# A three-block fp32 network: spectra swapped, maxima spread and a taps' spectrum doubled by DMA instead of TensorE

## What is computed

```python
p = h @ w_in
a_val, a_gate, z_a, q, k, v, o, z_b, gates = split_cols(p, EVEN_SIZES)
u = a_val * jax.nn.sigmoid(a_gate)
u = depthwise_conv_centred(u, conv_w, conv_b)          # 31 taps per channel
u = jax.nn.silu(group_layer_norm(u, gn_g, gn_b, A_GROUPS))
y_a = u * jax.nn.silu(z_a)
h_fwd = mlstm_chunkwise(qh, kh, vh, i_f, f_f)          # 4 heads, and again backwards
h_bwd = fl(mlstm_chunkwise(fl(qh), fl(kh), fl(vh), fl(i_b), fl(f_b)))
y = jnp.concatenate([y_a, y_b], axis=-1) @ w_out
```

## Time and profile before

| | us |
|---|---|
| three runs | 868.88, 870.31, 870.93 |
| median | 870.31 |
| the profiled execution, its time | 870.27 |
| its span on the core | 868.5 |
| PE busy | 850.9 |
| DVE busy | 500.8 |
| ACT busy | 476.6 |
| POOL busy | 38.5 |

### The profile page before, as it was taken

How to read it: one execution, slowest core, us unless ns; L and a number is a source line. 1 busy time by engine, 2 the same in 40 slices (tenths; PEclk the granted TensorE clock), 3 DMA queues, 4 the chain that set the end, 5 groups by cost and what they waited for, 6 DMA issues and landing times.

```text
span 868.5 us, 10829 instructions
## 1 busy us (share of the span) xinstructions
PE 850.9 (98%) x4078; PEld 695.5 (80%) x4078; DVE 500.8 (58%) x759; ACT 476.6 (55%) x761; POOL 38.5 (4%) x67
## 2 busy tenths in 40 slices
PE   8999899999999999999999999999999999999996
PEld 6888787888888888887788766888888887788885
DVE  6657642656666666545355644856665566546463
ACT  6557645663456555433466463438764577555551
POOL 2000000000000000810000010000000100000000
PEclk9999999999999999999999999999999999999999
DMA  8763433655466565675456514535564557265021
GB/s 270 257 190 117 146 97 98 193 172 188 129 197 216 175 186 191 175 240 189 152 178 200 169 33 162 170 98 170 171 219 155 145 171 248 73 184 192 2 97 48
DMA packets 75876, 140.36 MB, mean 162 GB/s; under 512 B 6082, under 2 KB 12517, under 8 KB 75825
## 3 DMA queue, kind: packets, MB, share of 16 engines
q1 hardware_dynamic: 72432, 134.37, 49.2%
q0 software_dynamic: 3328, 5.29, 2.2%
q10 hardware_dynamic: 64, 0.02, 0.0%
HBM read 138.56 MB, written 1.06 MB: 161 GB/s over the span
## 4 chain that ended last, share of the span: by engine, by line
PE 90%; DVE 4%; ACT 3%; issue 1%; DMA 1%; SPq 0%; DVEq 0%; ACTq 0%
PE acc L1552 25%; PE acc L1554 25%; PE acc L1553 25%; PE aux L1588 2%; PE aux L1840 2%; PE aux L1905 1%; DVE wlo L388 1%; ACT whi L534 1%; PE aux L2024 1%; PE aux L1968 1%; PE aux L1829 1%; DMA raw<-in_w_in 1%; PE aux L2032 1%; PE aux L2033 1%; PE aux L1701 1%
## 5 line engine op out<-in xcount | busy, mean ns | idle before, releaser
L388 DVE TENSOR_TENSOR wlo<-raw,whi 128x1024 fp32r<-128x1024 f32 (+2 forms) x257 | 304.7, 1203 | 228.6 <-ACT whi L534 227.9
L534 ACT ACTIVATE whi<-raw 128x1024 fp32r<-128x1024 f32 (+2 forms) x257 | 264.4, 1045 | 232.6 <-PE acc L1554 208.9
L1552 PE MATMUL acc<-whi,a_hi 128*128 128x512 f32 (+4 forms) x720 | 277.5, 385 | 3.3 <-DVE wlo L388 2.5
L1554 PE MATMUL acc<-whi,a_lo 128*128 128x512 f32 (+4 forms) x720 | 272.7, 379 | 0.0
L1553 PE MATMUL acc<-wlo,a_hi 128*128 128x512 f32 (+4 forms) x720 | 272.2, 378 | 0.0
L1552 PEld LDWEIGHTS acc<-whi,a_hi 128*128 128x128 f32 x720 | 135.8, 189 | 33.0 <-issue 5.4
L1554 PEld LDWEIGHTS acc<-whi,a_lo 128*128 128x128 f32 x720 | 135.6, 188 | 24.9
L1553 PEld LDWEIGHTS acc<-wlo,a_hi 128*128 128x128 f32 x720 | 135.8, 189 | 24.2 <-issue 0.7
L1552 PE MATMUL acc<-whi,b_hi 128*128 128x512 f32 x234 | 92.3, 395 | 0.1
L1554 PE MATMUL acc<-whi,b_lo 128*128 128x512 f32 x234 | 91.2, 390 | 0.0
L1553 PE MATMUL acc<-wlo,b_hi 128*128 128x512 f32 x234 | 91.1, 389 | 0.0
(11 more groups left out here) (334 smaller groups left out, 774.6 us busy)
## 6 DMA issues: line engine op xcount, KB each, us to landing
raw<-in_even_w_in SPq DMA_DIRECT2D x54, 512.0 KB, 4.4
raw<-in_w_in SPq DMA_DIRECT2D x50, 512.0 KB, 3.8
raw<-in_w_up SPq DMA_DIRECT2D x32, 512.0 KB, 4.5
raw<-in_w_down SPq DMA_DIRECT2D x32, 512.0 KB, 3.5
raw<-in_even_w_out SPq DMA_DIRECT2D x16, 512.0 KB, 4.1
raw<-in_odd_w_in SPq DMA_DIRECT2D x16, 512.0 KB, 4.5
raw<-in_odd_w_out SPq DMA_DIRECT2D x12, 512.0 KB, 3.7
raw<-in_w_branch_gla SPq DMA_DIRECT2D x8, 512.0 KB, 3.3
```

The source lines that it names most:

```text
L388: return e.tensor_tensor(w_view(wlo[u % SPLIT], u), w_view(raw[u % RAW], u), w_view(whi[u % SPLIT], u).bitcast(F32), ALU.subtract)
L534: act.activation(w_view(whi[u % SPLIT], u), w_view(raw[u % RAW], u), ACT.Copy).then_inc(sem("hi_done"), 1)
L1552: pe.matmul(acc_of(c, t), ah[:, ts], hi[:, k], start=first, stop=False)
L1554: ins = pe.matmul(acc_of(c, t), al[:, ts], hi[:, k], start=False, stop=last)
```

## The change

- **Taps' spectrum.** FW keeps one matrix of 128 columns (cosines, then sines). PE makes two matmuls instead of four. ACT copies rows 0 to 63 of each bank (real part) to rows 0 to 63 of WS[:, 0], rows 64 to 127 (imaginary part) to SOB and, negated, to rows 64 to 127 of WS[:, 1]. POOL issues four transfers that fill the other halves of the rows (ws_in).
- **Spectra.** ACT copies each of the three banks of a way there to `spectrum(b, 0)` (`spectra_out`). POOL issues for each block two transfers that put its halves, exchanged, into `spectrum(b, 1)` (`swap_halves`). The DVE waits for these, multiplies both by WS in SBUF and adds the second to the first (three more instructions for each n). The way back has one matrix FI and four matmuls instead of eight, and waits for `filtered`. FI's loads are halved.
- **Maxima.** POOL writes RM to the DRAM tensor `skew` and reads it back into MB on 128 partitions (1 MB; MB lies in EQT). ACT waits for it (mb_in) and reads MB instead of the banks. PE's four matmuls with 4 rows go, and "eq" is one piece.
- **Order.** The way back 1 on PE stands behind the turn of the keys; `conv_rows(1)` on the DVE behind three units of "ev1"; `filtered(1)` behind all of pump("eq"); the DVE splits one unit of "eq" ahead of `filtered(0)`; `group_rstd(1)` on ACT stands behind the copies of "ev1".

```diff
--- before.py
+++ after.py
@@ -150,10 +150,10 @@
         if STAGES >= 2:
-            AUX += [("ws", w, n) for w in range(2) for n in range(2)] + split_keys("en", 8) + [("gat", 0), ("gat", 1)]
+            AUX += [("ws", n) for n in range(2)] + split_keys("en", 8) + [("gat", 0), ("gat", 1)]
             AUX += [("fx", 0, b) for b in range(3)] + [("cvT", 0, t) for t in range(NT)] + [("mcol",)]
-            AUX += [("mb", h) for h in range(4)] + [("fx", 1, b) for b in range(3)]
-            AUX += [("eqT", 0, j) for j in range(2)] + [("cvT", 1, t) for t in range(NT)] + [("eqT", 1, j) for j in range(2)]
+            AUX += [("fx", 1, b) for b in range(3)]
+            AUX += [("eqT", w, j) for w in range(2) for j in range(2)] + [("cvT", 1, t) for t in range(NT)]
             AUX += [("kq", h) for h in range(4)]
@@ -266,18 +266,19 @@
             FT = sb("FT", [P, 4, 2 * P], c=c3)
-            FI = sb("FI", [P, 2, 4, P], c=c3)
+            FI = sb("FI", [P, 4, P], c=c3)
             cvb = sb("cvb", [P, D], c=c3)
...
             e_hi, e_lo = sb("e_hi", [P, 4, TOK], F32R, c=c3), sb("e_lo", [P, 4, TOK], F32R, c=c3)
+            MB = flat(EQT[:, :, :, :]).rearrange("p (h d t) -> p h d t", h=4, d=2)
             HM = flat(EQK[:, :, :, :]).rearrange("p (t n) -> p t n", t=NT)
...
             wcv_in = SOB[0:31, 0]
-            FW = SOB[0:31, 1, 0:512].rearrange("p (w c) -> p w c", w=2)
+            FW = SOB[0:31, 1, 0:256]
@@ -474,24 +475,42 @@
                 chain(pool.memset(FT[:, :, :], 0.0))
-                chain(pool.memset(FI[:, :, :, :], 0.0))
+                chain(pool.memset(FI[:, :, :], 0.0))
                 pool.dma_start(wcv_in, A["even_conv_w_2"][0]).then_inc(sem("wcv_in"), 16)
                 rows = A["dft_s"].rearrange("n (a c) -> n a c", a=2)
-                for a in range(2):
-                    pool.dma_start(FW[:, :, P * a:P * a + P], rows[0:31, :, 0:P]).then_inc(sem("wcv_in"), 16)
+                pool.dma_start(FW.rearrange("p (a c) -> p a c", a=2), rows[0:31, :, 0:P]).then_inc(sem("wcv_in"), 16)
                 for j, (_, p0, r0, n) in enumerate(F_ROWS):
...
                 for j, (p0, m0, n) in enumerate(I_COLS):
-                    for w in range(2):
-                        for a in range(2):
-                            pool.dma_start(FI[64 * a:64 * a + 64, w, j, p0:p0 + n], odd[0:64, 1, (a + w) % 2, m0:m0 + n]
-                                           ).then_inc(sem("fi_in"), 16)
+                    for a in range(2):
+                        pool.dma_start(FI[64 * a:64 * a + 64, j, p0:p0 + n], odd[0:64, 1, a, m0:m0 + n]
+                                       ).then_inc(sem("fi_in"), 16)
                 pool.dma_start(gbias[:, :], A["even_b_gate_2"][0].partition_broadcast(P)).then_inc(sem("gbias_in"), 16)
                 pool.dma_start(cvb[:, :], A["even_conv_b_2"][0].partition_broadcast(P)).then_inc(sem("cvb_in"), 16)
+                for n in range(2):
+                    aux_done(pool, ("ws", n))
+                    cs = slice(512 * n, 512 * n + 512)
+                    pool.dma_start(WS[64:128, 0, cs], WS[0:64, 0, cs]).then_inc(sem("ws_in"), 16)
+                    pool.dma_start(WS[0:64, 1, cs], SOB[64:128, 0, cs]).then_inc(sem("ws_in"), 16)
                 pool.wait_ge(sem("units_used"), CH[CI["dn1"]]["units"][-1] + 1)
...
                 pool.dma_start(gnb[:, :], A["even_gn_b_2"][0].partition_broadcast(P)).then_inc(sem("gn_in"), 16)
+                def swap_halves(n):
+                    for b in range(3):
+                        aux_done(pool, ("fx", n, b))
+                        for a in range(2):
+                            own, other = slice(64 * a, 64 * a + 64), slice(64 - 64 * a, 128 - 64 * a)
+                            pool.dma_start(spectrum(b, 1)[other], spectrum(b, 0)[own]).then_inc(sem(f"swapped{b}"), 16)
+
+                swap_halves(0)
+
+                pool.wait_ge(sem("m_rows"), 1)
+                pool.dma_start(A["skew"][0, 0:4], flat(RM)).then_inc(sem("rm_out"), 16)
+                pool.wait_ge(sem("rm_out"), 16)
+                rows = bass.AP(tensor=A["skew"].tensor, offset=A["skew"].offset, ap=[[0, P], [512, 4], [1, 512]])
+                pool.dma_start(MB.rearrange("p h d t -> p h (d t)"), rows).then_inc(sem("mb_in"), 16)
+
                 for h in range(4):
@@ -499,6 +518,7 @@
                                            ).then_inc(sem("dw_masked"), 1)
+                swap_halves(1)
                 aux_wait(pool, ("num", 3, 1, 1))
@@ -713,17 +733,11 @@
                 for n in range(2):
-                    key = ("ws", 0, n)
+                    key, cs = ("ws", n), slice(512 * n, 512 * n + 512)
                     aux_wait(act, key)
-                    aux_free(act.activation(WS[:, 0, 512 * n:512 * n + 512], bank(key)[:, :], ACT.Copy, scale=64.0), key)
-                for n in range(2):
-                    key = ("ws", 1, n)
-                    aux_wait(act, key)
-                    for a in range(2):
-                        rows = slice(64 * a, 64 * a + 64)
-                        ins = act.activation(WS[rows, 1, 512 * n:512 * n + 512], bank(key)[rows, :], ACT.Copy,
-                                             scale=(-64.0, 64.0)[a])
-                    aux_free(ins, key)
+                    act.activation(WS[0:64, 0, cs], bank(key)[0:64, :], ACT.Copy, scale=64.0)
+                    act.activation(SOB[64:128, 0, cs], bank(key)[64:128, :], ACT.Copy, scale=64.0)
+                    aux_free(act.activation(WS[64:128, 1, cs], bank(key)[64:128, :], ACT.Copy, scale=-64.0), key)
             pump("dn1", 3)
@@ -773,6 +787,18 @@
                     copy_out("ea1", AV[:, t, 512:1024], t, scale=rms(2, t))
+
+                def spectra_out(n):
+                    if n == 1:
+                        aux_done(act, ("cvT", 0, 0))
+                        aux_done(act, ("cvT", 0, 1))
+                    for b in range(3):
+                        key = ("fx", n, b)
+                        aux_wait(act, key)
+                        aux_free(act.activation(spectrum(b, 0), bank(key)[:, :], ACT.Copy), key)
+
+                act.wait_ge(sem("ws_in"), 64)
+                spectra_out(0)
                 pump("eb1")
@@ -780,17 +806,17 @@
                 act.activation(flat(mcol[:, 1]), flat(mcol[:, 1]), ACT.Exp, scale=-1.0).then_inc(sem("clamp"), 1)
+                act.wait_ge(sem("mb_in"), 16)
                 for h in range(4):
-                    aux_wait(act, ("mb", h))
                     for d, st, o, a, n in BLOCKS:
-                        ins = act.activation(DW[:, h, d, o:o + n], halves(("mb", h))[:, d, a:a + n], ACT.Relu,
+                        ins = act.activation(DW[:, h, d, o:o + n], MB[:, h, d, a:a + n], ACT.Relu,
                                              bias=mcol[:, 0, d, st, h:h + 1])
-                    aux_free(ins, ("mb", h))
-                    aux_done(act, ("mb", h))
+                    chain(ins)
                     act.activation(flat(DW[:, h]), flat(DW[:, h]), ACT.Exp, scale=-1.0).then_inc(sem("dw_exp"), 1)
...
                     copy_out("eq", EQK[:, 0, t], t, scale=rms(2, t))
+                spectra_out(1)
                 pump("ek")
@@ -841,10 +867,10 @@
                 turned_heads(1)
+                pump("ev1")
+                for t in range(NT):
+                    copy_out("ev1", EV[:, t, 2:4, 0:256], t, scale=rms(2, t))
                 group_rstd(1)
-                pump("ev1")
-                for t in range(NT):
-                    copy_out("ev1", EV[:, t, 2:4, 0:256], t, scale=rms(2, t))
                 for h in range(4):
@@ -1227,14 +1253,16 @@
                 def filtered(n):
-                    for w in range(2):
-                        aux_done(dve, ("ws", w, n))
+                    cs = slice(512 * n, 512 * n + 512)
+                    dve.wait_ge(sem("ws_in"), 64)
                     for b in range(3):
-                        key = ("fx", n, b)
-                        aux_wait(dve, key)
+                        dve.wait_ge(sem(f"swapped{b}"), 32 * (n + 1))
                         for w in range(2):
-                            ins = dve.tensor_tensor(spectrum(b, w), bank(key)[:, :], WS[:, w, 512 * n:512 * n + 512], ALU.mult)
-                        aux_free(ins, key)
+                            ins = dve.tensor_tensor(spectrum(b, w), spectrum(b, w), WS[:, w, cs], ALU.mult)
+                    chain(ins)
+                    for b in range(3):
+                        dve.tensor_tensor(spectrum(b, 0), spectrum(b, 0), spectrum(b, 1), ALU.add
+                                          ).then_inc(sem("filtered"), 1)
@@ -1320,6 +1348,7 @@
                 pump("ea1")
+                pump("eb1", 1)
                 filtered(0)
@@ -1329,14 +1358,12 @@
                 group_stats(0)
-                pump("eq", 3)
+                pump("eq")
                 filtered(1)
-                pump("eq")
-                pump("ek", 3)
-                conv_rows(1)
```

(34 more changed lines are left out.)

## The result

The changed kernel takes 866.18 us (median of 20 runs, 864.39 to 870.49) against 870.80 (20 runs, 868.82 to 874.53): ratio 0.9949, interval [0.9938, 0.9961]. It is faster by 4.6 us, not by the 11.9 forecast, and lies 2.2 us above the range. Its profiled execution took 864.44 us, next to the fastest of the 20, with a span of 862.7 against 868.5.

A forecast was written before the change was run, and what follows sets the result against it. PE, busy 98% of the span, was taken to bound the kernel. 870.3 less 14.4 us of PE time plus a 2.5 us stall gave 858.4 us, range 855.4 to 864.0.

The forecast's parts named there:

- What PE loses: PE time taken off: taps 1.92, ways back 6.87, spread maxima 3.93, half clock 1.70; 14.4 us in all.
- The clock: Half clock at 514.3 to 517.6, taken as caused by the four-row spread matmuls; 1.70 us gained when they go.
- L: Time from a POOL issue's end to landing of 128 KB between partitions beside weights; 4 us, ends 2.7 and 8.
- both stalls: PE waits for swapped spectra: 0 us after the first way there, 2.5 us before the first "ev0" product.
- the formulas: Stall by landing time L: max(0, L - 5) at the first way there, about L - 1.6 at the second.
- The half clock behind the stall: Slow PE clock after its wait before "ev0"; not in the forecast sum, only a rival of 1.7 us, 10%.
- longer landings: Rival: L near 8 beside weight loads, stalls 3 and 6.4 us, 865.3 us in all; 13%.
- the throttle: Rival: the stall puts PE at half clock for a stretch, 1.7 us more, 860.1 us; 10%.
- Hidden: Work said to cost PE nothing: taps' transfers, maxima through memory, second way back, ACT's moved rstd.
- three signs of being wrong: Wait before "ev0" missing or above 6 us, ACT held past 504 by the maxima, or PE waiting for loads.
- the prediction's case without a stall: Rival: early landing or DVE finding the pairs ready, so no new PE wait; 855.9 us, 10%.

The follow-up runs named there:

- the maxima alone: Kernel before with only the maxima's write and read through memory, the four spread matmuls gone; 865.30 us, ratio 0.9931.
- The loads held: Changed kernel with SyncE holding the loads of "ev0" units 1 to 3 until the second six swaps have landed; 859.98 us, ratio 0.9867.
- The idle turns: Changed kernel with 36 transposes of the identity on PE ahead of the first product of "ev0"; 864.39 us, ratio 0.9933.
- the filter behind "ev0": Changed kernel with filtered(1) on the DVE behind the low parts of "ev0" instead of ahead of them; 858.43 us, ratio 0.9845.
- the first loads held: Changed kernel with filtered(1) behind "ev0"'s low parts, plus SyncE holding loads from "eq" unit 2 until the first six swaps landed; 856.49 us, ratio 0.9842.
- the filter by blocks: Changed kernel with filtered(1) behind "ev0"'s low parts, plus the DVE's filter in two steps, blocks 0 and 1 first; 856.65 us, ratio 0.9850.
- the swaps by ScalarE: Changed kernel with the twelve swaps issued by ScalarE behind each of its copies instead of by POOL; 867.96 us, ratio 0.9967.
- blocks alone: Changed kernel with the DVE's filter in two steps, filtered(1) in its old place; 865.46 us, ratio 0.9947.
- the spectra alone: Changed kernel with the four spread matmuls back on PE and no maxima through memory; 867.76 us, ratio 0.9963.

## Why the prediction was wrong, step by step

- **What PE loses** was right. Taps 1.72 us (two of 1.92 to two of 1.06) for 1.92; ways back 6.63 for 6.87; from the end of the mcol transposes to the second way there 16.7 us before, 11.1 after, so 5.6 for 3.93 + 1.70. Together 13.9 for 14.4.
- **The clock** was right: the maxima alone keep it at 1.00, and putting the matmuls back alone brings two stretches of half clock.
- **L** was wrong: it is the term that was mis-sized. I took 4 us for the landing "under a second stream of weights", from two rows for 128 and 124 KB, and gave L near 8 only 13%. It measured 6.9 us from the issue's start in the first stretch and 6.0 to 6.4 in the second: 6.4 and 5.5 to 5.9 from its end. The two rows were indeed taken beside other traffic, at shares of 0.82 and 0.91; what they lacked were five more swaps on top of the loads (1.18 MB in flight beside the 128 KB, and not 2.88). The loads held show the cause (6.0 to 2.7 us). The taps' transfers, with the DMA engines nearly idle near 415, took 2.2 to 2.5 us.
- The fit of the Trainium skill ("DMA: Bandwidth & Descriptors", section "Anatomy of one DMA — SWDGE (gpsimd) path") gives 128 KB an estimate of 2.3 us. The trace agrees with it near 415; beside the weights the landing is nearly three times that.
- **The places of both stalls, and the formulas,** were right. They give 6.4 - 5 = 1.4 us and 3.9 to 4.3 us for these landings; measured 1.64 and 4.30, where the forecast had 0 and 2.5. By these landings alone the time would be about 861.6, inside the range, whose end was L = 7.3. In the second are also four times 0.14 us of ScalarE's reads from SBUF, which I had put at PSUM's price.
- **The half clock behind the stall** is the second step that failed: the forecast had it at nothing, as a rival of 10%, from one wait of 2.3 us that left the clock at 1.00. The changed kernel's wait was 4.3, so that row was no bound for it. In the profiled execution it cost 1.70 us, as priced (nearer 1.5, since PE still waits in its first 0.4 us). Behind the waits of 3.30 and 5.18 us in other kernels it lasted 6.8 us, an estimate of 3 us lost. The idle turns show that PE's doing nothing in the wait brings it.
- The Trainium skill ("TensorE: Matmul & The Clock Gate", section "HAM oscillation — how this bites in real kernels") says that waits between groups of matmuls can drop the clock each time. Here it dropped behind 4.30 us and not behind 1.64.
- Two rivals, longer landings and the throttle, therefore came true together: 855.9 + 1.64 + 4.30 + 1.70 = 863.5, against 864.4 of the profiled execution (0.5 of the rest is the 14.4 that was 13.9). I had priced them one at a time and never their sum, though they hang together: the throttle came with the longer wait. For L = 8 the sum would have been 865.3 + 1.7 = 867.0, which the range left out.
- The rest of the 1.7 us up to the median is of the size of more half clock, but where it falls is not shown, since only one execution of the changed kernel was profiled. Its mean granted clock is 0.996; the median of the 20 is 0.993 and the lowest 0.989, and 0.003 of 863 us is an estimate of 2.6 us more lost to the clock. In the kernel with the filter behind "ev0" the median is 0.9975 and with the first loads held 0.9985, which also fits their larger gains. Two ways to more half clock are in the traces: about 3 instead of 1.7 us behind the second stall, and some behind the first, which ranges from 0.85 to 2.15 us in five kernels whose work on PE, ScalarE and the DVE is the same up to there.
- **Hidden** were, as said: the maxima's way through memory (its 1 MB landed in 4.9 us, at about 499, against 502.8 wanted; the write ahead of it is 8 KB, not 16, and took 7.3 us, not 3.1), the taps' transfers, the second way back, ScalarE's moved rstd. None of the three signs of being wrong that I had named came (a second wait missing or above 6 us, ScalarE held past 504, PE waiting for loads), though the time left the range. A small slip: by the two formulas the gain is used up at L = 10.5, not 10.6.

The versions that beat both kernels are the changed one with `filtered(1)` behind the low parts of "ev0" and either the filter by blocks (856.65) or the first loads held (856.49). Both stand within 0.8 us of the prediction's case without a stall, 855.9. The two together were not tried.

## What to carry to other kernels

A transfer that takes the place of a matmul is priced by its landing beside the transfers that run at that moment, not by its size. A low DMA share tells an idle stretch (2.2 us here), but a full one can mean 4 us or 6: add up the bytes that will be in flight together, its siblings and the loads. Divided by the GB/s of such a stretch they say when the whole lot has landed, 10 us here. Where a queue is in order, put the work that the bottleneck wants next (here the low parts of weights) ahead of any wait for such a transfer; here that was worth 7.8 us, against the 4.6 of the whole change without it. And price a new wait of PE together with the half clock that may follow it.

## What was not expected of the hardware

- Half clock follows a wait of PE in some executions and not in others. Waits of 1.64, 1.61 and 1.53 us did not bring it; of 2.12 and 2.15 us did, for 1.7 us lost; the wait of 2.3 us near 94, which every kernel has, left the clock alone in nine profiled executions and brought it down in three (the filter by blocks, from 98 to 102, the swaps by ScalarE, and blocks alone, from 96 to 100). Behind 4.30 us it lasted 3.4 us, behind 3.30, 5.03 and 5.18 about 7, and it began before these waits ended.
- A transfer of 8 KB landed in 1.7 us where no swap was in flight (maxima alone), in 1.8 where ScalarE issued the swaps (and this write came ahead of them), and in 7.3 behind six swaps in POOL's queue.
- The same two pairs of four-row matmuls brought half clock once in the kernel before, behind the second pair, and behind both in the spectra alone (one execution of each was profiled).
